# Four weight pairs of the attention output projection, split once and kept in HBM as two parts

## The reference

```python
h = x @ w_in                                  # layer 0: q, k, v, gate
...
out = (silu(g) * r) @ w_out
x = post_norm(x, out, ln_gain[0], ln_bias[0])
kv = x @ swa_w_kv                             # one K/V for layer 1
h = x @ swa_w_in                              # q, gate
o = softmax(q k^T + bias, with a sink) v      # window of 128
out = (o * silu(gate)) @ swa_w_out            # the output projection of this case
x = post_norm(x, out, ln_gain[1], ln_bias[1])
```

## Time and profile before

| | |
|---|---|
| three runs | 2463.83, 2468.54, 2475.05 us, median 2468.54 |
| the profiled execution | 2462.66 us, its span 2460.7 us |
| mean granted TensorE clock | 0.983 |
| busy: PE, PE weight load, DVE, ACT, POOL | 95%, 77%, 74%, 48%, 14% |
| HBM read, written | 379.75 MB, 57.41 MB |
| output projection, pairs SO to SO + 13 | from 630.3, 1222.5, 1814.8 and 2396.3 us on |

### The profile page before, as it was taken

One profiled execution on the slowest core, in us unless ns is written; L12 is line 12 of the kernel. 1 busy time (PEld: TensorE's weight loads), 2 busy tenths in 40 slices (PEclk: granted clock), 3 DMA queues, 4 the chain that ended last, 5 costly groups with the idle time before them and its releaser, 6 DMA issues.

```text
span 2460.7 us, 30984 instructions
## 1 busy us (share of the span) xinstructions
PE 2330.8 (95%) x11506; PEld 1898.8 (77%) x11506; DVE 1815.1 (74%) x2578; ACT 1178.9 (48%) x1754; POOL 346.2 (14%) x352
## 2 busy tenths in 40 slices
PE   6889989889999999999999999999999999999995
PEld 5777777767778888787777888878777888888774
DVE  7877888755887677885597776886579667787457
ACT  3433345336544445534744444553664445553473
POOL 4212201112011100111210011100111110010122
PEclk9999999999999999999999999999999999999998
DMA  9787667581564345745275544585247344464413
GB/s 330 275 304 253 225 238 245 170 288 56 189 238 137 129 155 167 234 157 179 73 238 186 168 147 134 167 269 165 97 146 258 121 140 158 129 211 129 131 59 113
DMA packets 215061, 443.38 MB, mean 180 GB/s; under 512 B 15040, under 2 KB 52432, under 8 KB 211328
## 3 DMA queue, kind: packets, MB, share of 16 engines
q1 hardware_dynamic: 200832, 375.58, 46.8%
q0 software_dynamic: 14080, 65.83, 7.3%
HBM read 379.75 MB, written 57.41 MB: 178 GB/s over the span
## 4 chain that ended last, share of the span: by engine, by line
PE 69%; DVE 13%; DMA 9%; ACT 4%; issue 3%; SPq 1%; POOL 0%; POOLq 0%; DVEq 0%; ACTq 0%
PE accs L647 19%; PE accs L648 18%; PE accs L649 18%; DMA stage<-t_prep 5%; DVE w_lo L1254 4%; PE bank L647 2%; PE bank L649 2%; PE bank L648 2%; ACT w_hi L951 2%; DMA stage<-swa_w_in 2%; PE bank L888 1%; PE bank L869 1%; PE bank L878 1%; PE bank L733 1%; ACT pr L1212 1%
## 5 line engine op out<-in xcount | busy, mean ns | idle before, releaser
L1254 DVE TENSOR_TENSOR w_lo<-stage,w_hi 128x1024 fp32r<-128x1024 f32 x536 | 669.8, 1254 | 394.9 <-ACT w_hi L951 393.6
L951 ACT ACTIVATE w_hi<-stage 128x1024 fp32r<-128x1024 f32 x536 | 563.7, 1057 | 610.9 <-DMA stage<-t_prep 271.2
L647 PE MATMUL accs<-w_hi,xs 128*128 128x512 f32 x1120 | 448.8, 401 | 48.7 <-ACT sg L956 13.1
L649 PE MATMUL accs<-w_hi,xs 128*128 128x512 f32 x1120 | 441.6, 394 | 0.0
L648 PE MATMUL accs<-w_lo,xs 128*128 128x512 f32 x1120 | 441.4, 394 | 0.0
L647 PEld LDWEIGHTS accs<-w_hi,xs 128*128 128x128 f32 x1120 | 213.3, 190 | 102.3 <-issue 54.0
L647 PE MATMUL accs<-x_hi,w_hi 128*128 128x512 f32 (+1 forms) x640 | 247.7, 387 | 15.3 <-DVE qT L1724 14.3
L1848 POOL TENSOR_TENSOR rstd<-ve,half 128x1 f32<-128x1 f32 x96 | 81.1, 845 | 1193.7 <-DVE ve L1310 1145.2
L649 PEld LDWEIGHTS accs<-w_hi,xs 128*128 128x128 f32 x1120 | 213.4, 191 | 45.7
L648 PEld LDWEIGHTS accs<-w_lo,xs 128*128 128x128 f32 x1120 | 213.4, 191 | 42.4
L648 PE MATMUL accs<-x_lo,w_hi 128*128 128x512 f32 (+1 forms) x640 | 239.2, 374 | 0.0
(11 more groups left out here) (184 smaller groups left out, 3876.9 us busy)
## 6 DMA issues: line engine op xcount, KB each, us to landing
stage<-t_prep SPq DMA_DIRECT2D x224, 512.0 KB, 4.5
stage<-ret_w_in SPq DMA_DIRECT2D x96, 512.0 KB, 3.9
stage<-ret_w_in SPq DMA_DIRECT2D x128, 256.0 KB, 2.9
stage<-swa_w_in SPq DMA_DIRECT2D x64, 512.0 KB, 4.5
t_prep<-t_buf POOLq DMA_DIRECT2D x28, 1024.0 KB, 6.0
stage<-ret_w_out SPq DMA_DIRECT2D x48, 512.0 KB, 3.7
cs<-rope_t SPq DMA_DIRECT2D x16, 1024.0 KB, 7.4
t_buf<-ret_w_in POOLq DMA_DIRECT2D x32, 512.0 KB, 9.5
```

Of the source, the lines that this page charges most:

```text
L647: mm(dst, lhs[0], rhs[0], start=start, stop=False, skip_group_check=reopened)
L649: return mm(dst, lhs[1], rhs[0], start=False, stop=stop, skip_group_check=reopened)
L951: copy(w_hi[:, g % HS], stage[:, g % LS], ACT.Copy).then_inc(w_hi_made, 1)
L1254: nc.vector.tensor_tensor(w_lo[:, g % LS], stage[:, g % LS], w_hi[:, g % HS].bitcast(F32), sub).then_inc(w_split, 1)
```

## The change

```diff
-KEPT_IN = {}
+KEPT_IN = {SO + 5: 0, SO + 7: 0, SO + 9: 0, SO + 11: 0}
 KEPT = sorted(KEPT_IN)
```

## The result

The changed kernel took 2503.29 us, the median of four runs (2492.81 to 2514.44), beside 2471.11 us for four runs of the kernel before: a ratio of 1.0127 with a 95% interval of 1.010 to 1.0153, slower by 32 us. The forecast was 2486.5, 18 us slower, with a range up to 2497, and the measured time lies above that range; the direction and the two mechanisms held, the size did not. The profiled execution is the longest of the four, 2514.44 us with a span of 2512.4 us, so its stages add up to more than the medians differ by.

The account below looks back on a forecast made before the run. TensorE and VectorE were taken as almost level in the output projection, with DMA well used. Block 0's stores (13 us) plus later blocks' loads (5.3) made 18.3; 18 on the median 2468.54 gave 2486.5 us, range 2464 to 2497.

Parts of the forecast that it names:

- What bounds the stage: Output projection: TensorE and VectorE almost level, DMA well used; removing stops that VectorE causes gives at most 6.9 us.
- the stop at s6: First pair of P5, blocks 1 to 3: 1.41 us stop on L1465 stays; the pair starts 0.1 us later.
- Block 0, 13 us late: Output projection: loads and high parts wait for landed stores; delays of 3.0, 5.6, 8.2, finally 13 us.
- stores wait their turn: Block 0, SP's queue: stores wait behind x loads, 1.5 us each, so the first pair is stored at 654.9.
- the stop at s8: First pair of P7, block 0: starts 3.0 us late behind the first stores; TensorE waits 4.6 us.
- Blocks 1 to 3, 5.3 us: Output projection: late ordinary loads outweigh the saved low parts; 5.3 us lost together in these blocks.
- every ordinary pair after a kept one lands 2.8 us later: Blocks 1 to 3: ordinary load is third in its group, 1.25 us per transfer ahead; VectorE waits for it.
- my 6.5: Blocks 1 to 3: third load of a group is in 6.5 us after the first issue, against 3.7 alone.
- Stores pass the loads: Rival, block 0: stores overtake queued x loads, only 2 us lost there plus 5.3, so 2476; chance 0.20.
- Relief decides: Rival, blocks 1 to 3: third load at most 1.3 us late, up to 6.9 us back, 2463.6; chance 0.15.
- The clock: Rival, block 0: two waits above 3 us each bring 3.4 us at half clock; 2494; chance 0.10.
- The mean rate as the bound: HBM rule of about 358 GB/s: ordinary load 3.2 us late instead of 2.8, sum some 2 us larger; not adopted.

Follow-up runs that it names:

- The relief alone: Changed kernel without stores, and in blocks 1 to 3 the kept pairs neither split nor loaded, multiplied with whatever lies in the buffers; 0.9963 against the kernel before.
- a new order: Kernel before, nothing kept; on VectorE the sums of four output projection steps go ahead of the low part of the pair three later; 0.9964, 2457.86 us.
- Stores only: Changed kernel with block 0's stores kept, but the later blocks split every pair as before; 1.0062 against the kernel before, 16.4 us slower.
- the stores that nobody waits for: Block 0's eight stores take the rope tables instead of the parts, waits for them removed, later blocks split as before; 1.0016 against the kernel before, 2.6 us slower.
- ordinary load first: Changed kernel, but SP issues the ordinary pair of a step ahead of the kept one; 1.0085 against the kernel before, 21 us slower.
- Loads only: Changed kernel without stores; blocks 1 to 3 load two 512 KB arrays from the stored sums of x in the same steps; 1.0057 against the kernel before.
- the filler: Transposes of a constant tile in TensorE's waits; for block 0, 76 added to "Stores only": 1.0049 against the kernel before, beside 1.0062 without.
- its filled form: "Loads only" with 20 and 32 TensorE transposes of a constant tile ahead of s6 and s12 in blocks 1 and 2; 1.0058 against the kernel before.
- the last experiment: Changed kernel with the sums ahead of the low part on VectorE in four output projection steps; 1.0124 against the kernel before, 28 us slower.

## Why the forecast was right in its direction and short in its size

**What bounds the stage: right.** VectorE's order in front of the bank sums causes the stops. The relief alone takes them away (6.65 us of waits, 6.9 forecast), and so does a new order. The signs that I had named came: 524 high and low parts, first stores of 8.9 and 9.5 us to landing, stops of 4.46, 3.62 and 3.61 us in and behind block 0's stage, the stop at s6 still there and a new one at s12, with VectorE idle on the high part ahead of both.

**Block 0, 13 us late: right, slightly small.** "Stores only" has 16.4 us on its time, and in its profile 11.5 us on the stage and 5.7 behind it. The step-by-step positions hold at first: the first store pair landed 10.1 us after its first issue, as "stores wait their turn" has it (I had 10.4), and the stop at s8 is 4.46 us where I had 4.6. In the changed kernel s8, s10, s12 and the last stop, at block 1's first banks, are 2.8, 6.0, 9.9 and 14.5 us late, where I had 3.0, 5.6, 8.2 and 13. That it is the wait and not the bytes is shown by the stores that nobody waits for: 42.8 us for the stage. What the sum left out is the clock, which falls with the waits, and what follows. I wrote that nothing more is lost after that last stop; of the 17.2 us of "stores only" 14.4 are lost up to it and 2.8 behind it. SP enters block 1 with its lead gone; whether that or the clock takes the 2.8 us is not shown.

**Blocks 1 to 3, 5.3 us: wrong, and this is the step that failed.** The sentence was "every ordinary pair after a kept one lands 2.8 us later", from 1.25 us for each transfer ahead. The place was right (ordinary load first: 41.4 and 42.0 in blocks 1 and 2), and so was the chain from the landing to the stop. The size was not: third loads landed 6.3 to 8.1 us after the first issue at s6 and 8.6 to 8.9 at s12, so 2.6 to 5.2 late against a lone load. Put the measured landings into my own steps and they come out right. At s6 my 6.5 gave a stop of 1.5 us (the old 1.41 and 0.1); with 8.12, 7.18 and 6.26 it gives 3.1, 2.2 and 1.3, and 3.15, 2.22 and 1.30 were measured. At s12 of block 1 my 6.5 gave a stop of 1.8 us, so 8.7 gives 4.0; it was 4.95, and the 1.0 us that I had as a stop at s10 was no longer there to hide part of it.

The rate had come from one group of the earlier trace rows. The same page of before has all transfers of that kind:

```profile
xs<-x_sums SPq DMA_DIRECT2D x24, 512.0 KB, 6.4
```

Their median is 6.4 us to landing and the slowest took 9.2, beside the 5.6 of the one I used. The 24 are not alike, though: up to six transfers are in flight when one is issued. The second of two such loads behind a weight load took 5.7, 5.6 and 5.5 us where nothing followed for 4.8 us or more, and 6.4, 7.9 and 6.3 where SP issued a store 0.5 us behind it. So the row that I used was typical of its place and not of a place with traffic behind it, and that was there to be read. The changed kernel fits this at s6: 8.1 and 7.2 us with two x loads right behind, 6.3 without. In the three other kernels with ready loads first it is 6.7 to 7.4 with them and 6.2 to 6.8 without. That what is issued behind a load can delay it is my reading of these rows; no run varies it alone.

The stages lost 10.5, 8.4 and 5.2 us in the profile of the change, 24.1 in all, against 5.3. Of the 24.1, 13.7 are more idle time of TensorE and 10.4 are matmuls at the lower clock, a term that the main sum put at nothing and left to a rival of 0.10. "Loads only" lost 14.0 us in its profile and 15.4 in time.

**The sum.** In the timed runs stores and loads cost 16.4 and 15.4 us (each within some 5), together 31.8, beside the 32.2 of the whole change. The forecast had 13 and 5.3. Ten of the missing 14 us are the loads', three or four the stores'.

**The rivals.** *Stores pass the loads*: fell, 8.9 and 9.5 us to landing. *Relief decides*: fell; its own condition, a third load late by no more than 1.3 us, was never met. Yet that the order of two VectorE instructions gives the whole relief at no cost was not among the things I weighed. *The clock*: it was given 0.10 and two stretches; half the time at 0.50 comes to 18.7 us in the four stages of the changed kernel's profile. The rival's own estimate, two stretches, was too low by far; with 25.2 us it came nearer to the 32 measured than the forecast's 18. In block 0 the filler gave back 2.2 of 6.8 us, since the next wait, at s10, grew by 2.4; so waits and clock loss are not simply to be added there. For blocks 1 to 3 the tests leave it open.

**The mean rate as the bound.** In the changed kernel two stretches of block 1 read:

```profile
1267.00:1273.80 6.80, 5.66 (x13) 4.45 (x14) 5.45 (x5) 2.00 (x2) 0.00 (x0) 0.50 1.04 395
1290.90:1297.70 6.80, 5.34 (x13) 4.26 (x14) 6.80 (x9) 0.52 (x1) 0.00 (x0) 0.50 0.00 0
```

The first row moves 395 GB/s for 6.8 us. The Trainium skill, DMA: Bandwidth & Descriptors (where 436 GB/s comes from), lets HBM bind at about 358; this trace is above it on a core that works alone. The rule would have put the ordinary load 3.2 us late instead of 2.8, nearer to what was measured, but for a reason that the row doesn't bear out: the late transfers are late one by one, not by a bound on the mean rate. While the late group of s12 was under way, from 1276.5 to 1281.0, the DMA engines moved 218 GB/s.

**What stays open.** What makes the group at s12 late. Twelve such groups are in the four profiles with ready loads first (the change, "loads only", its filled form and the last experiment). In six SP's second issue took 0.86 to 1.55 us and the third load was in after 7.8 to 8.9 us; in the other six it took 0.43 to 0.55 us and the third load came after 6.4 to 7.4. Beside each of those six late groups the profile has a transfer of 16 KB on its instruction queue (q8), within half a microsecond of the group's first issue; but two of the other six have one too, just before it. No run here moves that transfer away, so it is a suspicion. And how much of the 15 us of the loads is the fallen clock.

## What to carry to other kernels

Before taking work away from an engine that others wait for, look at what it does just ahead of the result they wait for: here four low parts moved behind the sums gave 0.9964, and taking twelve away by way of HBM gave 1.0127. A store that must land before its slot is reused makes the queue that issues it wait behind every prefetch already in flight, and on another queue it still competes with them (1.0027 against 1.0085); an extra prefetch is paid by the load issued behind it. When a step of a forecast rests on the time of one transfer, look at all of its kind, sort them by what stands ahead and behind, and carry the latest of them through the sum as the end of a range. And when an edit moves work, check in which blocks that work still exists.

## What the hardware showed unexpectedly

**A wait of some three microseconds costs a second time.** In the changed kernel the four stages have six waits over 3 us, and a seventh of 3.61 stands right behind block 0's; with each goes a stretch of 3.4 or 6.8 us at a granted clock of 0.50 (1.2 GHz), and so it does with one wait of 2.22 us in block 2; in the other kernels waits of 1.8 to 2.0 us are found both with such a stretch and without; the two rows above are the stretches after s6 (3.15 us) and s12 (4.95 us) of block 1. Filler transposes in place of the waits kept the clock at 1.00 in the stages that had them. The Trainium skill, TensorE: Matmul & The Clock Gate (the HAM clock gate), has an idle array fall to 1.2 GHz and return with sustained work; the trace agrees. What the filler showed besides is that the higher clock gave back only 2.2 us, up to the start of block 1's stage, of the 6.8 us of clock loss that were gone.

**Two issuing engines are one set of DMA engines.** With the stores on GpSimd's queue an SP load took 13.7 us, the longest in this stage of any kernel here, against 7.8 before, and two stores issued behind it on the other queue landed 2 to 4 us ahead of it. The Trainium skill, DMA: Bandwidth & Descriptors (issuing engines are not separate DMA queues), says that transfers of all issuing engines run on the same DMA engines and interleave; this load bears it out.
